# One hybrid decoder layer on one core: expert weights moved as pairs of slots, 16 KB per partition, with rows turned to match

## The reference

```
h = rmsnorm(x);  p = h @ w_in                                # six parts of 1024 columns
y_a = (gelu(u) * (W_s v + b_s)) @ w_branch_a                 # chunks of 128 positions, v = layernorm(gelu(.))
y_b = silu(layernorm(conv31(c_val * sigmoid(c_gate)))) @ w_branch_b + b
x = x + (sigmoid(g_a) * y_a + sigmoid(g_b) * y_b) @ w_out
h = rmsnorm(x);  logits = h @ w_router + b_router            # 32 experts, the 4 largest, softmax over them
gu = h[rows of e] @ w_up[e] + b_up[e]                        # 1024 x 2048 each
act = (clip(up) + 1) * min(gate, 7) * sigmoid(1.702 * min(gate, 7))
y = x + sum over the chosen e of weight * (act @ w_down[e] + b_down[e])    # 1024 x 1024 each
out = rmsnorm(y) * norm_final_g                              # and two convolution states, chunk_v of the sample
```

## Time and profile before

| | |
|---|---|
| median of three runs | 1279.13 us (1275.46 to 1279.46) |
| profiled execution, its own time | 1276.55 us |
| its span | 1274.8 us |
| granted TensorE clock, mean | 0.984 |
| TensorE matmul / weight load busy | 91% / 45% of the span |
| DVE / ScalarE / GpSimd busy | 42% / 19% / 51% |
| DMA | 94581 packets, 449.06 MB, mean 352 GB/s |
| SP's queue / GpSimd's queue | 345.88 MB / 101.52 MB |

### The profile page before, as it was taken

How to read it: one execution, slowest core, us unless ns; L and a number is a source line. 1 busy time by engine, 2 the same in 40 slices (tenths; PEclk the granted TensorE clock), 3 DMA queues, 4 the chain that set the end, 5 groups by cost and what they waited for, 6 DMA issues and landing times.

```text
span 1274.8 us, 30490 instructions
## 1 busy us (share of the span) xinstructions
PE 1155.6 (91%) x11113; PEld 578.5 (45%) x11114; DVE 540.6 (42%) x1161; ACT 242.6 (19%) x483; POOL 650.7 (51%) x743
## 2 busy tenths in 40 slices
PE   8999999999999889888898998998988889889886
PEld 7877777775434333333233433333333333333232
DVE  1999984122633233433332343332333233323424
ACT  2012124000222122122122221221212111222122
POOL 0022300000566766857862678577576765756863
PEclk9999999999999999999999999998999999999998
DMA  9983433642899999999998999999999999999993
GB/s 261 341 272 109 135 131 135 264 168 101 354 422 402 422 421 422 422 422 421 422 422 374 367 407 422 422 422 422 422 415 422 422 422 422 421 422 422 422 421 153
DMA packets 94581, 449.06 MB, mean 352 GB/s; under 512 B 8526, under 2 KB 42894, under 8 KB 45339
## 3 DMA queue, kind: packets, MB, share of 16 engines
q1 hardware_dynamic: 79918, 345.88, 68.1%
q0 software_dynamic: 13872, 101.52, 19.3%
q10 hardware_dynamic: 749, 1.19, 0.3%
HBM read 447.00 MB, written 2.42 MB: 353 GB/s over the span
## 4 chain that ended last, share of the span: by engine, by line
PE 41%; DMA 27%; DVE 13%; POOL 8%; issue 8%; POOLq 1%; ACT 1%; DVEq 0%; SPq 0%; ACTq 0%
DMA ring<-in_w_down 19%; PE banks L1392 13%; DVE arena L815 8%; DMA arena<-in_w_up 8%; PE banks L1405 8%; PE banks L1190 8%; POOL ring L526 7%; PE banks L1105 3%; PE banks L1306 2%; PE banks L1170 2%; PE banks L1142 2%; PE banks L1179 1%; PE banks L1149 1%; POOL ring L528 1%; DVE arena L824 1%
## 5 line engine op out<-in xcount | busy, mean ns | idle before, releaser
L1392 PE MATMUL banks<-ring,hT 128*32 128x512 f32 x3328 | 419.2, 603 | 44.6 <-POOL ring L528 32.9
L526 POOL COPY ring<-arena 128x1024 f32<-128x1024 f32 x279 | 291.2, 1044 | 129.8 <-POOLq L520 127.4
L528 POOL COPY ring<-arena 128x1024 f32<-128x1024 f32 x279 | 292.6, 1049 | 36.9 <-POOL ring L526 0.9
L1405 PE MATMUL banks<-ring,hT 128*32 128x256 f32 x3328 | 224.4, 389 | 45.2 <-DMA ring<-in_w_down 44.9
L345 DVE TENSOR_TENSOR xq<-xq,banks 128x256 f32<-128x256 f32 x53 | 22.3, 421 | 500.7 <-PE banks L1179 500.7
L1392 PEld LDWEIGHTS banks<-ring,hT 128*32 128x32 f32 x3328 | 98.2, 110 | 203.6 <-issue 96.4
L1190 PE MATMUL banks<-hT,ring 128*128 128x288 f32 x768 | 190.5, 409 | 0.0
L1405 PEld LDWEIGHTS banks<-ring,hT 128*32 128x32 f32 x3328 | 101.3, 111 | 185.8 <-issue 78.6
L532 POOL DMA_DIRECT2D ring<-in_w_down x96 | 50.8, 529 | 257.3 <-POOLq L520 142.6
L1190 PEld LDWEIGHTS banks<-hT,ring 128*128 128x128 f32 x768 | 146.4, 192 | 40.2
L783 DVE TENSOR_SCALAR WT<-slot_ids,prod 128x128 f32 x153 | 86.6, 622 | 62.3 <-PE banks L1105 62.0
(11 more groups left out here) (250 smaller groups left out, 817.1 us busy)
## 6 DMA issues: line engine op xcount, KB each, us to landing
arena<-in_w_up SPq DMA_DIRECT2D x248, 1024.0 KB, 14.1
ring<-in_w_down POOLq DMA_DIRECT2D x96, 1024.0 KB, 11.4
arena<-in_w_down SPq DMA_DIRECT2D x31, 1024.0 KB, 16.2
ring<-in_w_in SPq DMA_DIRECT2D x24, 1024.0 KB, 10.2
ring<-in_w_up SPq DMA_DIRECT2D x8, 1024.0 KB, 4.8
ring<-in_w_branch_b SPq DMA_DIRECT2D x4, 1024.0 KB, 4.9
ring<-in_w_branch_a SPq DMA_DIRECT2D x4, 1024.0 KB, 4.8
ring<-in_w_out SPq DMA_DIRECT2D x4, 1024.0 KB, 4.9
```

The costliest lines, as they stand in the source:

```text
L526: nc.gpsimd.tensor_copy(ring[:, k, 0:D], parked[k][:, 0:D]).then_inc(half_copied, 1)
L528: nc.gpsimd.tensor_copy(ring[:, k, D:SLOT], parked[k][:, D:SLOT]).then_inc(slot_full[k], 16)
L1392: ins = mm(UP[g * BLK:(g + 1) * BLK, :], xT[:, k, :], ring[:, k, g * 512:(g + 1) * 512], start=k == 0, stop=k == UP_SLOTS - 1)
L1405: ins = mm(DN[q * BLK:(q + 1) * BLK, 0:256], actT[:, f % 4, f // 4, :], ring[:, UP_SLOTS + j, h * D + q * 256:h * D + (q + 1) * 256], star ...
```

## The change

All expert weights move in pairs of neighbouring slots, 2 MiB in one transfer with 16 KB per partition. Partition p of a pair of up slots holds rows 2p and 2p+1 of 256; of a pair of down slots four neighbouring rows. Ten slots (five pairs) are staged, the pair 10 and 11 is direct. SP waits for the copy of the second slot of a pair before it loads the pair again. GpSimd still copies slot by slot, now in plain order 0 to 9, and then issues the one direct load.

The rows of the activations must match: `turn_rows` reads the gathered rows at a stride of two, `turn_raw` and the turning of b_up at a stride of four, and `take_x` multiplies by the norm's weights in pair order. These come by one more small transfer of ScalarE (4 rows x 1 KB into a free region), two more small transposes, and a ninth column of `cols`. To make room for the tenth parked slot, hT moves into the arena behind the mixing tensors, the final norm's weights go into parked slots 2 and 3 at the end (loaded by SP after the loop, no longer by ScalarE), and the temporaries share memory: xg and lin are one buffer, gs and sg another.

At the start of the expert stage SP loads parked pairs (0, 1) and (2, 3), then ring pairs 0, 2, 4, 6 (each after two mixing blocks), parked pair 4 between them, parked pair 6, ring pair 8 at `mo_ready` 5, and parked pair 8 only after the router's last logits, whose input it overwrites.

```diff
-PARKED = 9
+PARKED = 10
-TURNS = [0, 1, 2, 3, 4, 5, 6, 7, 9, 8, 10, 11]
+DIRECT = 10
...
-        def weights(e, k):
+        def pair_weights(e, k):
             if k < UP_SLOTS:
-                return a["w_up"][0, bass.ds(e, 1), k * P:(k + 1) * P, :].rearrange("e p n -> (e p) n")
+                return a["w_up"][0, bass.ds(e, 1), k * P:(k + 2) * P, :].rearrange("e (p h) n -> p (e h n)", p=P)
             j = k - UP_SLOTS
-            return a["w_down"][0, bass.ds(e, 1), j * 256:(j + 1) * 256, :].rearrange("e (p h) n -> p (e h n)", p=P)
+            return a["w_down"][0, bass.ds(e, 1), j * 256:(j + 2) * 256, :].rearrange("e (p h) n -> p (e h n)", p=P)
...
-            for k in range(EARLY_SLOTS):
-                load_parked(1, k)
-            for k in range(UP_SLOTS):
+            for k in (0, 2):
+                load_parked_pair(1, k)
+            for k in range(0, UP_SLOTS, 2):
                 sp.wait_ge(*mix_block_used(MIX_BLOCKS - SLOTS + k))
-                load_slot(0, k)
-                if k == 3:
-                    load_parked(1, EARLY_SLOTS)
+                sp.wait_ge(*mix_block_used(MIX_BLOCKS - SLOTS + k + 1))
+                load_pair(0, k)
+                if k == 2:
+                    load_parked_pair(1, 4)
             sp.wait_ge(ya_evac, 2 * KC)
...
+            load_parked_pair(1, 6)
+            sp.wait_ge(mo_ready, 5)
+            load_pair(0, UP_SLOTS)
+            sp.wait_ge(logits_ready, NT)
+            load_parked_pair(1, UP_SLOTS)
...
-                load_parked_again(place + 1, after, STAGED)
+                for k in range(0, DIRECT, 2):
+                    sp.wait_ge(slot_full[k + 1], place * 16 + 16 * FILLS)
+                    load_parked_pair(after, k)
+            sp.wait_ge(slot_full[3], (NE - 1) * 16 + 16 * FILLS)
+            load(fing, a["norm_final_g"].rearrange("(l d) -> l d", l=1).to_broadcast([P, D]), fing_in)
...
-                pool.wait_ge(parked_full[k], 16 * e)
+                pool.wait_ge(parked_full[k - k % 2], 16 * e)
...
-                for n, k in enumerate(TURNS):
-                    wait_used(before, k, (e - 1) * SLOTS + n)
-                    if k in STAGED:
-                        copy_slot(e, k, STAGED.index(k))
-                    else:
-                        load_slot(here, k)
+                for k in range(PARKED):
+                    wait_used(before, k, (e - 1) * (PARKED + 1) + k)
+                    copy_slot(e, k, k)
+                wait_used(before, SLOTS - 1, (e - 1) * (PARKED + 1) + PARKED)
+                load_direct(here)
...
-                V.tensor_tensor(xT, XB[:, 256:512].rearrange("p (k t) -> p k t", k=KC),
-                                cols[:, NORM_FFN, :].unsqueeze(2).to_broadcast([P, KC, BLK]), ALU.mult
+                V.tensor_tensor(xT.rearrange("p (j h) t -> p j h t", h=2),
+                                XB[:, 256:512].rearrange("p (j h t) -> p j h t", j=4, h=2),
+                                pair_cols.unsqueeze(3).to_broadcast([P, 4, 2, BLK]), ALU.mult
...
+                pairs = xg.rearrange("t (p h) -> t h p", h=2)
                 for h in range(2):
-                    ins = tr(turned[:, h], xg[:, h * P:(h + 1) * P])
+                    ins = tr(turned[:, h], pairs[:, h])
...
-                pairs = raw.rearrange("t (b p h) -> t b h p", h=2, p=P)
+                fours = raw.rearrange("t (p h) -> t h p", h=4)
                 for c in range(4):
-                    ins = tr(TB[:, c * P:(c + 1) * P], pairs[:, c // 2, c % 2])
+                    ins = tr(TB[:, c * P:(c + 1) * P], fours[:, c])
```

More of the change, by code:

```diff
@@ L152, in hybrid_layer @@
         R1, R2, R4, R3 = (region(KC * T) for _ in range(4))
-        fing = arena[:, PARKED * SLOT:PARKED * SLOT + D]
+        assert taken[0] == MIX_ARENA
+        hT_flat = region(KC * T)
+        hT = hT_flat.rearrange("p (k t) -> p k t", k=KC)
+        fing, fingq = parked[2][:, 0:D], parked[3][:, 0:256]
         def view(t, c):
@@ L187, in hybrid_layer @@
         xT = carve("hT", KC * BLK).rearrange("p (k t) -> p k t", k=KC)
-        raw, lin = carve("hT", 512), carve("hT", 256)
-        xg, sg, gs = (carve("hT", 256) for _ in range(3))
+        raw, sg = carve("hT", 512), carve("hT", 256)
+        xg, lin, gs = lin[:], lin[:], sg
         actT = carve("hT", 256).rearrange("p (c q t) -> p c q t", c=4, q=2)
@@ L223, in hybrid_layer @@
         slot_full = [sem(f"slot_full{k}") for k in range(SLOTS)]
[L224 removed]
+        direct_full = sem("direct_full")
         parked_full = [sem(f"parked_full{k}") for k in range(PARKED)]
@@ L401, in _, with load_pair, load_parked_pair @@
                 load_block(n)
[L403 to L415, removed]
+            def load_pair(e, k):
+                sp.dma_start(ring_pair(k), pair_weights(e, k)).then_inc(slot_full[k], 16)
+            def load_parked_pair(e, k):
+                sp.dma_start(arena[:, k * SLOT:(k + 2) * SLOT], pair_weights(e, k)).then_inc(parked_full[k], 16)
             sp.wait_ge(sp_evac, 2 * G)
             sp.wait_ge(v_stored, 16)
-            for k in range(EARLY_SLOTS):
-                load_parked(1, k)
-            for k in range(UP_SLOTS):
+            for k in (0, 2):
+                load_parked_pair(1, k)
+            for k in range(0, UP_SLOTS, 2):
                 sp.wait_ge(*mix_block_used(MIX_BLOCKS - SLOTS + k))
-                load_slot(0, k)
-                if k == 3:
-                    load_parked(1, EARLY_SLOTS)
+                sp.wait_ge(*mix_block_used(MIX_BLOCKS - SLOTS + k + 1))
+                load_pair(0, k)
+                if k == 2:
+                    load_parked_pair(1, 4)
             sp.wait_ge(ya_evac, 2 * KC)
-            for k in range(EARLY_SLOTS + 1, PARKED - 1):
-                load_parked(1, k)
-            sp.wait_ge(*mix_block_used(MIX_BLOCKS - SLOTS + UP_SLOTS))
-            load_slot(0, UP_SLOTS)
-            load_parked(1, PARKED - 1)
+            load_parked_pair(1, 6)
[3 more added lines that the diff above has]
+            load_parked_pair(1, UP_SLOTS)
             sp.wait_ge(before_known, 1)
@@ L435, in _ @@
                 after = sp.value_load(order[0:1, bass.ds(place + 1, 1)], min_val=0, max_val=NE - 1)
-                load_parked_again(place + 1, after, STAGED)
+                for k in range(0, DIRECT, 2):
[3 more added lines that the diff above has]
+            load(fing, a["norm_final_g"].rearrange("(l d) -> l d", l=1).to_broadcast([P, D]), fing_in)
+            for q in range(QN):
+                load(fingq[q * NS:(q + 1) * NS, :],
+                     a["norm_final_g"][q * 256:(q + 1) * 256].rearrange("(l d) -> l d", l=1).to_broadcast([NS, 256]),
+                     fing_in)
             for tt in range(NT):
@@ L528, in copy_slot, with load_direct @@
                 nc.gpsimd.tensor_copy(ring[:, k, D:SLOT], parked[k][:, D:SLOT]).then_inc(slot_full[k], 16)
-            def load_slot(e, k):
-                pool.dma_start(ring[:, k, :], weights(e, k)).then_inc(direct_full[DIRECT.index(k)], 16)
+            def load_direct(e):
+                pool.dma_start(ring_pair(DIRECT), pair_weights(e, DIRECT)).then_inc(direct_full, 16)
             pool.wait_ge(mo_ready, 5)
-            for k in DIRECT:
-                load_slot(0, k)
+            load_direct(0)
             pool.wait_ge(before_known, 1)
@@ L1111, in _ @@
                 if tt == 1:
-                    pe.wait_ge(vec_in, 16 * 8)
+                    pe.wait_ge(vec_in, 16 * 9)
+                    for h in range(2):
+                        tr(bank[7][:, 384 + 4 * h:388 + 4 * h], pair_rows[:, h])
                     tr(bank[7][:, 320:320 + 8 * KC], vecrows[:]).then_inc(pe_early, 1)
```

48 lines of the change are left out of this document (23 added, 25 removed).

## The result

The changed kernel takes 1298.59 us in the median (1298.02 to 1302.51), against 1277.89 us for the kernel before on the same chip: ratio 1.0173, 95% interval 1.0150 to 1.0196. It is slower, by some 22 us. The prediction, 1270.8 us with a range of 1259 to 1283, is wrong in sign. The profiled execution's span is 1300.8 us, 26.0 more than before.

The account below looks back on a forecast made before the run. Expert stage set by bytes over rate (421 GB/s), TensorE with slack; -7.1 - 1 - 3 - 1 - 1.3 + 2.2 + 1.9 + 1 = -8.3 us, on the median 1279.13 giving 1270.8 us, range 1259 to 1283.

Parts of the forecast that it names:

- The bound: Expert stage: DMA queues always hold work at 421 GB/s, so bytes over rate set the time and TensorE has slack.
- The prediction's own last test: If GB/s between 400 and 690 us rises over 1% and time does not fall, TensorE's claimed slack is wrong.
- Those are given back to the saturated stream, and are worth nothing by themselves.: Expert stage: TensorE's later waits on direct slots shrink, but this was priced at 0.
- part 3: Buffers and order: tenth parked slot against SP's later wait, -1 us; TensorE's first direct wait goes, -1.3; last burst held back, +2.2.
- so it is hidden: GpSimd's queue per burst: 22.1 us against 21.0 before, covered by 29.9 us of one expert's bytes; priced at 0.
- Lands 11.6 us on.: Direct pair in the expert stage: sharing engines equally, it lands 11.6 us after issue (4 x 2.49 + 1.6).
- Part 1: Expert weight stream: 16 KB packets save 5 to 37 ns per MiB, -7.1 us; fewer completion packets, -1 us.
- Part 2: Dry ends of DMA near 697 and 1244 us: one late engine improves with fewer GpSimd packets, -3 us (0 to 6.9).
- Part 4: Kernel's tail: last direct pair lands 7.5 us after a later issue, delaying the last down matmuls, +1.9 us (0 to 4).
- Part 5: Turned rows: transposes' weight loads go from packed, 137 ns, to strided, 201; 0.12 us per body, +1 us (0.5 to 4).
- rival A: Expert stream: every per-packet term at its upper end and late engine cured, -20.4 us, 1258.7 us, 427 GB/s or more; chance 0.16.
- Rival C: Burst starts: DMA runs dry because the first new pair is issued later, 2.2 us each; 1288 us; chance 0.16.

Follow-up runs that it names:

- e3: Changed kernel with every expert load single: parked slots one by one, direct pair split, 1 MiB each in 8 KB pieces; 1274.57 us, ratio 0.9983.
- e7: e2 with the direct pair, still one 2 MiB transfer, in pieces of 8 KB instead of 16 KB (rows not matched); 1296.04 us, ratio 1.0148.
- e6: Changed kernel with every pair, parked and direct, as one 2 MiB transfer in 8 KB pieces (rows not matched); 1305.63 us, ratio 1.0220.
- e2: Changed kernel with parked slots loaded one by one, 1 MiB in 8 KB pieces; direct pair stays one 2 MiB transfer; 1271.63 us, ratio 0.9957.
- e5: Changed kernel with parked pairs as 2 MiB transfers in 8 KB pieces (rows not matched), direct pair still 16 KB; 1279.89 us, ratio 1.0019.
- e8: e2, but SP waits for the copy of a pair's second slot before issuing both single loads; 1272.85 us, ratio 0.9977.
- e1: Changed kernel with the direct pair split into two 1 MiB transfers, 8 KB pieces, a semaphore each; parked pairs stay 16 KB; 1328.33 us, ratio 1.0400.
- e11: e3 with the parked slots in pieces of 4 KB, direct slots still 8 KB; 1291.32 us, ratio 1.0111.
- e12: e2 with the parked slots in pieces of 4 KB, direct pair still 16 KB; 1290.83 us, ratio 1.0108.
- e9: e2 with the direct pair issued ahead of the copies of slots 8 and 9 instead of behind them; 1269.66 us, ratio 0.9936.
- e4: Kernel before, with only w_up moved in pairs of 16 KB per partition, direct slots and order as before; 1322.69 us, ratio 1.0372.

## Why the prediction was wrong

**The bound.** "The expert stage is therefore set by bytes over rate; TensorE has slack there" is the step that failed, as a forecast of the changed kernel. Before, bytes and loop came out alike: the gathers at 459.59, 548.34 and 637.69 us are 88.8 and 89.4 us apart, three bursts each, and 36 MiB at 421 GB/s take 89.7. After, the same three (465.13, 557.01, 649.14) are 91.9 and 92.1 apart, though at 431 GB/s the bytes would take 87.6. TensorE had no slack to give to a later direct pair. The engines were full, but not with what was wanted next. The parked loads ran ahead (GpSimd waited 2.3 us for them in the whole kernel) and took half of the bandwidth from the direct loads, for which TensorE waited 44.9 us. The rows stood there, and I read them as "just in time" from the one chain row of the last burst. Elsewhere the chain went through the direct slots, in 15 places with 238 us in all. The prediction's own last test points the same way, if it is put to full windows: they rose by 2.1% and the time did not fall. By its letter, for the mean of 400 to 690 us, it does not apply, for that fell to 414.

**"Those are given back to the saturated stream, and are worth nothing by themselves."** This sentence of part 3 priced at 0 the term that made the result. A wait on a direct slot delays the gather, the next up slots, the next burst's copies, and with them the next direct issue: a loop. The pair put 2.6 us into it in the burst of the table. Another term at 0 lies in the same loop: GpSimd's longer turn, "so it is hidden" behind 29.9 us of bytes, is the first row of that table, 21.6 against 20.6 us. The experiments give the terms along one path, from ratios: a direct pair that lands whole +21.1 us (e3 to e7), parked pairs +9.2 (e7 to e6), 16 KB pieces -6.0 (e6 to after, the weak one), together +24.3 on e3's 0.9983. On another path the sizes differ: larger direct pieces alone are worth 24.4 us (e7 to e2), and parked pairs cost 7.9 us from e2 to e5. Why parked pairs cost 9.2 us is open: direct landings are 0.4 us later and waits 9.1 us longer, and SP's wait for the second copy cost 0.0020 in e8, but at another share.

**"Lands 11.6 us on."** Measured were 14.4 in the median, 7.9 at least. Equal sharing was right (213 of 426 GB/s), so 2 MiB need 9.8 us, and the rest of the landing is 4.6, where I had taken 1.6. I also took the landing of slot 11 as what counts, and did not ask at which slot the wait would then stand.

**Part 1** had the right direction, and its size in rate was above my upper bound: 431 against 422 GB/s, 52 ns per MiB where I gave 5 to 37. In time it was worth 6.0 us by e6 (7.1 forecast), where 52 ns for each of 336 MiB would be 17.5; that the two times agree is luck, since the rate was more than forecast and a loop, not the stream, set the time. **Part 2**: the tails are shorter, as its sign asked (16 GB/s from 706 to 708 us, 32 from 1269 to 1270.5, then none), but what that was worth in time can't be told. **Part 3's** first wait should have gone; it grew from 1.28 to 2.16 us, at down(2) instead of down(3). **Part 4**: the last direct load landed in 7.9 us (7.5 forecast) and split the last down matmuls by 0.93 us (2 forecast). **Part 5** held: the weight loads of the gathered rows are now

```profile
L1110 PEld LDWEIGHTS banks<-ident,lin x104: 193/206/224, 329.8 to 1258.2; 128*128 128x128 f32 x104
```

206 ns in the median (min/median/max in the row) where packed ones took 137, and one undisturbed body grew by 0.08 us, from 15.54 to 15.62 (gathers at 391.46 and 407.08 after). Two slips in the sums changed nothing in this: rival A takes 4 us for the completion packets, whose upper end is 7.9 (1254.8 us instead of 1258.7), and two thirds of 10 us are 6.7 and not 6.9.

**Rival C** came nearest by its sign (1288 us) and by its slices under 415 GB/s. Its mechanism, SP's wait for the second copy, was not the main cause: e7 has dips and most of the loss without it, and in e8 it cost 0.0020. As far as the engines idled, the likely reason is that all parked pairs had landed (GpSimd waited for none) and TensorE, held by the direct pair, freed nothing; that is argued from the waits, not shown. Rival A's rate ("427 or more") came in full windows only, without its time.

## What to carry to other kernels

Full DMA engines do not show that the rate alone will set the time after a change: look at whose landings the compute engines wait for, and at whose they don't. Where two queues shared the engines here, equal numbers of packets and not equal bytes went through (e1: 91 and 88 packets, 1.38 and 0.72 MB), so give the queue of the urgent load the larger pieces, issue it first, and leave the prefetch in smaller ones that still run near full rate (422 GB/s with 8 KB here; 4 KB cost more than they gave). Merging two loads into one also merges their completions, and it is the first consumer that pays.

## What was not expected of the hardware

The share by packets: 64.9% against 34.4% of the engines' time for 16 KB against 8 KB pieces, 32.4% against 71.0% the other way round. The rate by pieces: 412 GB/s with parked pieces of 4 KB, 422 with 8 KB and 431 with 16 KB. The mixing stage's 4 KB rows had shown 419; the flat 412 of e11 has them scattered in SBUF and mixed with 8 KB ones, and which of the two costs the difference was not tried (e12, mixed with 16 KB ones, had 412 as well). Behind all ten waits for direct slots of 3 us and more after, and behind six of the ten before (the earlier trace rows has one), TensorE went on at a lower granted clock (0.72 from 460 to 466 us), which cost 1.7 us behind the wait of 4.46. Yet a low mean clock is no sign of a slow kernel: the profiled e9, the fastest, has 0.962, as the profiled e4, one of the two slowest (after 0.968, before 0.984).
